# Experts' last rows of 64 or fewer: through raw weights in two column halves instead of a slot of their own

## The reference

```python
scores = sigmoid(xf @ router_w)                      # 1088 rows, 16 experts in 4 groups
# the best group, in it the 2 best experts; weights are their scores, normalised
hid = silu(xb @ w_gate[e]) * (xb @ w_up[e])          # 1024 -> 512, twice
yb = hid @ w_down[e]                                 # 512 -> 1024
out = zeros.at[token].add(yb * weight)
```

## Time and profile before

| | |
|---|---|
| median of 3 runs | 2472.15 us |
| span of the profiled execution | 2469.8 us |
| its mean granted TensorE clock | 0.958 |
| TensorE (products) busy | 2251.6 us, 91% |
| VectorE busy | 1330.9 us, 54% |
| ScalarE busy | 1097.6 us, 44% |
| DMA | 503.98 MB, mean 204 GB/s |
| weight loads of the experts | 96 of 2048 KB (32 experts by three) |

### The profile page before, as it was taken

How to read it: one execution, slowest core, us unless ns; L and a number is a source line. 1 busy time by engine, 2 the same in 40 slices (tenths; PEclk the granted TensorE clock), 3 DMA queues, 4 the chain that set the end, 5 groups by cost and what they waited for, 6 DMA issues and landing times. The chain is left out here.

```text
span 2469.8 us, 39160 instructions
## 1 busy us (share of the span) xinstructions
PE 2251.6 (91%) x11590; PEld 1673.2 (68%) x11590; DVE 1330.9 (54%) x2251; ACT 1097.6 (44%) x1870; POOL 326.6 (13%) x387
## 2 busy tenths in 40 slices
PE   7999997889689999999799999999989599999974
PEld 4766665667578888887486565656577488888851
DVE  4223212586766656663683443433367677755757
ACT  3221212642346655663443343434332266645645
POOL 0000002660011111010100433000000010100103
PEclk8999998999889999999899999999999699999987
DMA  7566655655558777785456544333261388866956
GB/s 281 175 209 218 224 190 166 188 178 197 177 206 296 274 251 278 275 292 178 143 169 203 183 147 139 94 103 102 90 214 43 134 319 317 315 230 222 321 196 225
DMA packets 194323, 503.98 MB, mean 204 GB/s; under 512 B 19152, under 2 KB 39089, under 8 KB 187696
## 3 DMA queue, kind: packets, MB, share of 16 engines
q1 hardware_dynamic: 165902, 409.88, 49.0%
q0 software_dynamic: 18416, 64.11, 7.5%
q10 hardware_dynamic: 9906, 28.75, 3.1%
HBM read 437.13 MB, written 73.42 MB: 207 GB/s over the span
## 5 line engine op out<-in xcount | busy, mean ns | idle before, releaser
L2260 DVE TENSOR_TENSOR e_wl<-e_raw,e_wh 128x1024 fp32r<-128x1024 f32 x384 | 452.2, 1221 | 117.2 <-ACT e_wh L2168 116.6
L2168 ACT CAST e_wh<-e_raw 128x1024 fp32r<-128x1024 f32 x384 | 379.4, 1048 | 84.7 <-DMA e_raw<-in_e_up 29.1
L2080 PE MATMUL e_psG<-e_wh,e_xh 128*128 128x512 f32 x784 | 320.5, 409 | 11.5 <-issue 7.4
L2082 PE MATMUL e_psG<-e_wh,e_xl 128*128 128x512 f32 x784 | 310.5, 396 | 0.0
L2081 PE MATMUL e_psG<-e_wl,e_xh 128*128 128x512 f32 x784 | 308.9, 394 | 0.0
L2080 PEld LDWEIGHTS e_psG<-e_wh,e_xh 128*128 128x128 f32 x784 | 147.8, 189 | 45.1 <-issue 12.9
L2082 PEld LDWEIGHTS e_psG<-e_wh,e_xl 128*128 128x128 f32 x784 | 147.4, 188 | 36.8
L2081 PEld LDWEIGHTS e_psG<-e_wl,e_xh 128*128 128x128 f32 x784 | 148.1, 189 | 31.4
L615 PE MATMUL in_ps<-in_w_upper,in_h_upper 128*128 128x512 f32 x384 | 155.3, 404 | 3.3 <-DVE in_h_lower L335 2.9
L2080 PE MATMUL e_psY<-e_wh,e_hh 128*128 128x512 f32 x392 | 155.6, 397 | 2.8 <-DVE e_hl L2283 2.8
L2082 PE MATMUL e_psY<-e_wh,e_hl 128*128 128x512 f32 x392 | 157.1, 401 | 0.0
(11 more groups left out here) (614 smaller groups left out, 4359.1 us busy)
## 6 DMA issues: line engine op xcount, KB each, us to landing
e_raw<-in_e_gate SPq DMA_DIRECT2D x32, 2048.0 KB, 11.7
e_raw<-in_e_up SPq DMA_DIRECT2D x32, 2048.0 KB, 9.1
e_raw<-in_e_down SPq DMA_DIRECT2D x32, 2048.0 KB, 8.1
x<-in_ada_w SPq DMA_DIRECT2D x40, 1024.0 KB, 5.3
yrows<-e_y ACTq DMA_DIRECT2D x49, 512.0 KB, 6.3
x<-in_cache SPq DMA_DIRECT2D x64, 320.0 KB
a_pages<-in_cache SPq DMA_DIRECT2D x64, 320.0 KB, 3.5
qkvo<-in_out SPq DMA_DIRECT2D x48, 256.0 KB, 2.3
```

Source lines behind the costliest of these rows:

```text
L2080: T.matmul(out, upper[:, k, :], wh[:, z, cols], start=k == 0, stop=False)
L2082: mm = T.matmul(out, lower[:, k, :], wh[:, z, cols], start=False, stop=k == PIECES * n - 1)
L2168: S.copy(wh[:, z, c * PC:(c + 1) * PC], raw[:, z, c * PC:(c + 1) * PC]).then_inc(s_hi[z], 1)
L2260: V.tensor_tensor(wl[:, z, at], raw[:, z, at], wh[:, z, at].bitcast(F32), ALU.subtract).then_inc(s_lo[z], 1)
```

## The change

An expert now gets a slot for its first 128 rows and one more for each further 128, but the last one only if it would hold more than 64 rows (`g.steps` becomes -1, 192, 320, ...). An expert's last 1 to 64 rows beyond its slots are a rest: they go with the expert's last slot, through the raw float32 weights, unsplit. TensorE's array is used in two column halves of 64: one product writes partitions 0 to 63 with the left half of the columns, the next writes 64 to 127 with the right half. Rests have places of their own in `yrows` behind the slots (PLACES = 48 blocks; SLOTS goes from 32 to 31). A table `g.slot_halves` counts the rests before each slot; `either` reads two neighbours of it and jumps to the body with a rest (`both`) or without (`whole`). `g.slot_fresh` goes: each slot loads and splits its own weights, an expert's second slot too. A raw weight's buffer is loaded anew only when the rest has used it (`s_rest`). More of `yrows` is filled ahead.

```diff
-SLOTS = (2 * N + E * (P - 1)) // P
-FULL = 2 * N // P
+ROWS = P // 2
+SLOTS = E + (2 * N - 3 * (ROWS + 1)) // P
+PLACES = SLOTS + E + 1
...
+        def either(eng, b, whole, both):
+            here, after = (table(eng, g.slot_halves, b + j) for j in range(2))
+            with eng.If(after > here):
+                both(here)
+            with eng.Else():
+                whole()
...
             def load(z, b):
-                with sp.If(table(sp, g.slot_fresh, b) > 0):
-                    e = table(sp, g.slot_expert, b) + layer * E
-                    sp.wait_ge(s_lo[z], b * PIECES + PIECES)
-                    fetch(z, e)
-                with sp.Else():
-                    sp.wait_ge(s_raw[z], b * 16)
-                    sp.sem_inc(s_raw[z], 16)
-                sp.drain()
+                e = table(sp, g.slot_expert, b) + layer * E
+                halves = table(sp, g.slot_halves, b)
+                sp.wait_ge(s_rest[z], halves)
+                sp.sem_inc(s_end, 1)
+                sp.wait_ge(s_lo[z], b * PIECES + PIECES)
+                fetch(z, e)
...
             def slot(b):
-                load(DOWN, b + 1)
-                load(UP, b + 2)
-                load(GATE, b + 3)
+                def gate_first():
+                    load(GATE, b + 1)
+                    load(DOWN, b)
+                def down_first(_):
+                    load(DOWN, b)
+                    load(GATE, b + 1)
+                either(sp, b, gate_first, down_first)
+                load(UP, b + 1)
...
+            def gather_rest(b, h):                     # POOL, before the rows of b + 1
+                take(h + (SLOTS - 1), 1)
+                po.wait_ge(s_xt, b + 1)
+                nc.gpsimd.indirect_dma_start(xg[0:ROWS, :], ...).then_inc(s_rx, 16)
...
+            def gate_up_rest(h):
+                pe.wait_ge(s_rxf, 2 * h)
+                pe.wait_ge(s_rout, h)
+                for z in (GATE, UP):
+                    for k in range(KD):
+                        for r, c in zip(column_groups(ROWS), column_groups(FE // 2)):
+                            mm = T.matmul(psS[r, z, :], xf[k // 4][:, k % 4, :],
+                                          raw[:, z, k * FE + c.start:k * FE + c.stop], start=(k == 0), stop=(k == KD - 1))
+                    mm.then_inc(s_rest[z], 1)
...
+            def down_rest(h):
+                pe.wait_ge(s_rhf, h)
+                out = psS[:].rearrange("p z f -> p (z f)")
+                for f in range(FT):
+                    for r, c in zip(column_groups(ROWS), column_groups(HALF)):
+                        mm = T.matmul(out[r, :], hf[:, f % 2, column_groups(ROWS)[f // 2]],
+                                      raw[:, DOWN, f * D + c.start:f * D + c.stop], start=(f == 0), stop=(f == FT - 1))
+                mm.then_inc(s_rest[DOWN], 1)
...
+            def with_rest(b, h, more=True):
+                turn_rest(h)
+                up(b)
+                gate_up_rest(h)
+                turn_hidden(b)
+                if more:
+                    turn_x(b + 1)
+                down(b, range(2))
+                turn_rest_hidden(h)
+                down(b, range(2, PIECES))
+                down_rest(h)
+                if more:
+                    pe.wait_ge(s_silu, b + 1)
+                    gate(b + 1, 0)
+                    gate(b + 1, 1)
...
+                def both(h):
+                    copy_rest(h)
+                    if not first:
+                        store(b - 1)
+                    renew(DOWN, b, b + 1)
+                    copy_hidden(b)
+                    silu_rest(h)
+                    act.wait_ge(s_xt, b + 2)
+                    act.wait_ge(s_used[UP], b + 1)
+                    copy_x(0)
+                    copy_x(1)
+                    copy_rest_hidden(h)
+                    renew(GATE, b + 1, b + 1)
+                    store_rest(b, h, y)
+                    renew(UP, b + 1, b + 1, range(2))
+                    act.wait_ge(s_rst, 32 * h)
+                    silu(b + 1)
+                    renew(UP, b + 1, b + 1, range(2, PIECES))
...
+            def with_rest(b, h):
+                multiply(b)
+                lower(DOWN, b, range(3))
+                lower_hidden(b)
+                lower(DOWN, b, range(3, PIECES))
+                multiply_rest(h)
...
+                def both(h):
+                    with_rest(b, h)
+                    lower_x(b + 1, 0)
+                    lower_x(b + 1, 1)
+                    lower(GATE, b + 1)
+                    lower(UP, b + 1)
```

More of the change, by code:

```diff
@@ L2024, in _ @@
             load(UP, 1)
-            load(GATE, 2)
             def slot(b):
-                load(DOWN, b + 1)
-                load(UP, b + 2)
-                load(GATE, b + 3)
-            slots(sp, slot)
+                def gate_first():
[6 more added lines that the diff above has]
+                load(UP, b + 1)
+            used = table(sp, g.slots_used, 0)
+            with sp.Fori(1, SLOTS - 1) as b:
+                with sp.If(used > b + 1):
+                    slot(b)
+                with sp.Else():
+                    sp.sem_inc(s_end, 1)
+            load(DOWN, used - 1)
             if layer == 0:
@@ L2109, in turn_hidden, with down @@
                 mm.then_inc(s_ht, 1)
[L2111 removed]
+            def down(b, pieces=range(PIECES)):
                 pe.wait_ge(s_hl, b + 1)
                 pe.wait_ge(s_out, b + 1)
[L2114 removed]
+                for c in pieces:
                     pe.wait_ge(s_lo[DOWN], b * PIECES + PIECES + c + 1)
@@ L2156, in _, with whole @@
             last = table(pe, g.slots_used, 0) - 1
-            up(last)
-            turn_hidden(last)
-            down(last)
+            def whole():
+                up(last)
+                turn_hidden(last)
+                down(last)
+            either(pe, last, whole, lambda h: with_rest(last, h, False))
         @block.scalar
@@ L2196, in store, with copy_rest @@
                 act.dma_start(g.yrows[bass.ds(b * P, P), :], y[:]).then_inc(s_st, 16)
-            def slot(b, first=False):
[L2199 to L2213, removed]
+            def copy_rest(h):
+                act.wait_ge(s_rt, h)
+                for j in range(2):
+                    S.copy(xf[j][:], psX[:, 4 * j:4 * j + 4, 0:ROWS]).then_inc(s_rxf, 1)
@@ L2231, in _ @@
             used = table(act, g.slots_used, 0)
[L2232 to L2235, removed]
+            slot(0, True)
             with act.Fori(1, SLOTS - 1) as b:
@@ L2241, in _, with whole, both @@
             last = used - 1
-            with act.If(used > 1):
-                store(act.value_load(g.slots_used[0:1, 0:1], min_val=2, max_val=SLOTS) - 2)
-            with act.Else():
+            def whole():
+                store(used - 2)
+                renew(DOWN, last, last + 1)
+                copy_hidden(last)
+            def both(h):
+                copy_rest(h)
+                store(used - 2)
+                renew(DOWN, last, last + 1)
+                copy_hidden(last)
+                silu_rest(h)
+                copy_rest_hidden(h)
+                store_rest(last, h, xg)
+                act.wait_ge(s_rst, 32 * h)
                 act.sem_inc(s_end, 1)
-            renew(DOWN, last, table(act, g.slot_fresh, last), last + 1)
-            copy_hidden(last)
+            either(act, last, whole, both)
             store(last)
@@ L2458, in _, with whole @@
             last = table(v, g.slots_used, 0) - 1
-            renew(DOWN, last, table(v, g.slot_fresh, last))
-            multiply(last)
-            lower_hidden(last)
+            def whole():
+                lower(DOWN, last)
+                multiply(last)
+                lower_hidden(last)
+            either(v, last, whole, lambda h: with_rest(last, h))
 def stage_combine(nc, g, layer, last):
```

222 lines of the change are left out of this document (154 added, 68 removed).

## The result

The changed kernel takes 2510.02 us in the median (2509.71 to 2516.31), the kernel before 2472.29 beside it: a ratio of 1.0156, with a 95% interval of 1.0139 to 1.0173. It is 1.6% slower where 2.3% faster was forecast, and the time lies 40 us above the range.

What follows compares the result with a forecast made beforehand. TensorE was taken to bound the expert slots, with loads a close second limit. Slot savings of -80.0 us and added costs of +22.4 gave -57.6, so 2414.5 us against the median of 2472.15; range 2365 to 2470.

Steps and rivals of the forecast that it cites:

- the routing: Ahead of the experts: more small VectorE steps, and tables ahead of the tokens, cost 2.5 us a layer, 5.0 in all.
- The later gather of the first rest: Slot 0's rest shares `xg`, so its gather starts some 1.5 us late: 3.0 us in all.
- A rest on TensorE: A rest's gate and up 3.35 us, down 1.7, with transposes 6.15 together; a slot with a rest 24.3 us of TensorE.
- A rule against it: Every slot's jump over one of two bodies would, by the instruction fetch rule, pay for fetches and make the sum slower.
- Rival 5: In the rests, column halves run one after the other: 5.0 us more per rest, 65 us, 2480 us; chance 0.02.
- R: A slot with a rest: 26.0 us, between 24.3 with all hidden and 29 with every load 3 us later.
- The wait for the rest's own store before SiLU: On ScalarE in a slot with a rest, waiting for that store costs 0 to 2 us.
- W1: A whole slot behind one with a rest: 25.0 us, with TensorE stalled 5.4 by a late gate load, plus 1.5 for clock.
- W: Other whole slots: 18.5 us in layer 0 and 19.0 in layer 1.
- The row of 19.2 us between gate loads: Three one-slot experts in a row: a slot with three own loads takes 19.2 us by its loads, 18.1 by TensorE.
- The turns: Skipped turns of the slots' loop, 0.9 us each on TensorE: 15 for 6 and 11 for 9, +8.1 and +1.8.
- Rival 6: Jumps in the expert slots cost instruction fetches of 1 to 6.0 us, once per slot: 2450 to 2630 us; chance 0.02.

Runs made afterwards that it cites:

- late wait: The change with ScalarE's wait for the landing of the rest's store moved from ahead of SiLU to ahead of the next write of y: 2485.55 us.
- best kernel: The change with later store wait, 19 loop turns, the body without a rest beside TensorE's last branch, and tables behind the tokens' step: 2459.5 us.
- 19 turns: The change with its slot loops cut from 30 turns to 19, enough for these inputs alone: 2489.55 us.
- near body: The change with 19 turns and, in TensorE's last block, the body without a rest placed directly behind its branch: 2487.44 us.
- no rests: The change with slot thresholds back at multiples of 128, so 26 and 23 slots, keeping own loads, new routing and new loop: 2515.85 us.
- no rests, 25 turns: The change with thresholds of 128, own loads, 25 loop turns and the body without a rest beside TensorE's last branch: 2505.67 us.

## Why the prediction was wrong

**The gap.** The profiled kernel was forecast at 2412.1 us and took 2508.1: 96 us more. From the router's first step to the first slot's transposes the two layers cost 7.9 us more than before, where the routing was put at 5.0. The later gather of the first rest was put at 3.0, and the rest's transposes come only 1.0 us later, both layers together, than the second slot's did before. Together that is 0.9 us more than forecast; most of the gap is in the slots.

**The step that failed** is "A rest on TensorE": "16 products (8 pairs) in 1.95 us". A product in fp32 takes two instructions, and the rows of the trace count instructions. It could have been read from the kernel before: L3500's loop makes 4 x 2 = 8 products and its row says x16. The 3.35 and 1.7 us of gate, up and down were 6.9 and 3.4; for 13 rests that is some 69 us of the 96. Halving the products bears it out with 4.3 us a rest. ("A rule against it" counts the two bodies' 218 products in the same way; they are 258 instructions.) Rival 5 gave the same doubled price to another mechanism (the column halves one after the other). That one is not what happened. A full-width fp32 product of 512 columns in the last stage of the changed kernel, in the timeline:

```profile
2478.25 1.02 PE L2740 MATMUL c_psN<-x,c_diagonal 128*128 128x512 f32 x2
```

One call, two instructions of 0.59 us each, so the second starts 0.43 us behind the first; the granted clock is 1.00 here. The 16 instructions of `down_rest`, as wide but in alternating column halves, take 3.65 us at the same clock. The trace has them in eight pairs: the two of a pair start 0.006 to 0.007 us apart, the pairs 0.43 to 0.48. So two instructions go in the time of one, and the halves do run together. A window of 0.02 us holds both starts of the first pair:

```profile
932.01 0.65 PE L2198 MATMUL e_psS<-e_raw,e_x_half_low 128*64 128x512 f32 x2
```

The right sum, 65 us more, stood in the text under the wrong cause and with 2 in 100.

**R behind R.** "The wait for the rest's own store before SiLU costs 0 to 2 us" was taken near nothing. The four such intervals are 33.3 to 34.9 us against 30.9 behind a whole slot: 14 us in all, shown by the late wait, which brings all four to 30.9 or 31.0. In slot R6 the 2.0 us gap in up costs another 1.75 us through the clock: nine products at about the spacing of 1.2 GHz, the lower level, so that 12 of them take 4.55 us for 2.8. The gap of 2.07 us in slot R7 didn't cost that.

**W1** was 27.3 us in the mean for a forecast 25.0: seven times 2.3 is 16 us. The stall itself was expected. What came on top was mostly the same store wait: with the late wait the seven take 25.1 to 26.5 us, 11 us less in all. So the step that was put at "0 to 2 us" cost 14 us in R behind R and 11 here, which is the 24.5 us that its removal gave. In the best kernel a W1 still takes 24.9 to 27.0 us, some 7 more than a plain whole slot, close to the 6.9 of the forecast. The forecast's reason, a gate load that is issued only when the last piece is lowered at the end of R, was not tried by itself.

**W** was over-priced: 18.2 us in layer 0 and 18.4 in layer 1 for 18.5 and 19.0, 9 us less over 16 slots. The row of 19.2 us between gate loads was taken for what the loads allow. But the DMA share rose to 1.04 with 396 GB/s, above the 373 of the earlier trace rows, and TensorE stayed busy for 99% of it.

**R itself**, once the products are right, was 31.3 by the prediction's sum and took 30.9: 5 us less over 13.

**The turns.** +8.1 and +1.8 became +9.7 and +7.2: the idle time ahead of the last slot went from 2.35 to 12.09 us in layer 0 and from 5.08 to 12.34 in layer 1, 7 us more than forecast. 3.9 us are the one long branch. The other 3 us were not traced to one cause. Rival 6, a fetch at every jump, did not come: within the loop of layer 0 the same branches take 0.33 us at most, as TensorE's row from 720 to 1140 us shows:

```profile
L2001 PEldq COMPARE_BRANCH  x22: 65/169/334, 734.8 to 1112.6; - x22
```

Once, behind the loop of layer 1, a long branch did come: 3.88 us in the change and 5.94 with 19 turns, each beside traffic on the instruction queue. With the near body it is gone, but the kernels without rests have one in the loop's first turn of layer 1, 6.22 and 6.61 us. That these are fetches is argued from the queue and from the length of the body jumped over; no run shows it directly. The Trainium skill (Runtime: NRT & Kernel Launch, Instruction fetch mechanics) has the rule that a taken branch out of the fetched window stalls; here the traces agree with it for single jumps over a long body, and not for the jumps of every slot.

These terms sum: 69 + 14 + 16 - 9 - 5 + 7 + 1 = 93 us of the 96. The other 3 are not assigned.

**What was right.** The slots of each layer and their order, the cost of routing and first gathers together (8.9 us for 8.0, by two errors that cancel), the 0.9 us of a turn, the direction of each stall, and the column halves side by side. The forecast of the sign failed on a price. A rest that costs 10.3 us of products leaves 13 x (18.2 + 18.2 - 30.9) = 72 us to be won, and the store wait, W1, the turns, the routing and the loads take it all: 14 + 7 x 9.1 = 78 us for the first two alone. With the store wait and the turns out of the way, the near branch and the tables moved back, 0.5% is left, and some 0.3% against a kernel before whose turns are cut as well.

## What to carry to other kernels

Before a duration is taken from a row, divide its instruction count by the calls in the source: a product in fp32 appears twice. A piece that is small on TensorE still brings its whole chain (a store to wait for, a load that may start only behind it); place its waits as late as the buffer allows, and price the chain ahead of the arithmetic. Empty turns of a loop with a fixed bound, and a jump over a long body at its end, are paid for here at about 0.9 us a turn and, for single jumps, 4 to 7 us.

## What the runs showed of the hardware

- A product in fp32 is two TensorE instructions, 64 for 32 calls in 7.1 us; instructions of 512 columns stand 0.43 us apart at full width, and in two column halves of 64 they start in pairs, 0.43 us from pair to pair: the halves run side by side.
- Weight loads of 2 MB reached a DMA share of 1.04 at 396 GB/s over 92 us and 1.03 at 395 GB/s over 380 us, with TensorE busy for 99%: the 1.00 at 373 GB/s of the earlier trace rows was not the limit.
- TensorE fell to the lower clock behind an idle stretch of only 2.02 us in a busy slot (nine products 0.35 to 0.43 us apart instead of 0.23), and did not behind one of 2.07 us in the next slot.
- Single branches of TensorE's sequencer over a long body took 3.88 us (the change), 5.94 (19 turns), 6.22 and 3.66 (no rests) and 6.61 (no rests, 25 turns). With the wanted body next to it the branch ahead of layer 1's last slot took 0.08 us and the jump behind that body 0.30, but without rests such a jump behind the body took 3.80 us in layer 0. The branches inside the loop of layer 0 took 0.07 to 0.33 us in the change.
